# A two-block transformer kernel on one core: where the AdaLN weights are summed, and the order of small work around the norms

## The chip, the cores and the metric

One core of one Trainium2 chip runs the whole program; seven cores stand idle. The metric is device time in microseconds (us) of one execution, median of the runs shown. All times in this text are us, unless ns is written.

## The reference, cut to what matters

The input x has 256 tokens (S) of 1024 features (D). The first block is a hybrid layer: an RMS norm, three branches (A: a gated linear recurrence; B: a sparse attention with a compressed key branch and a relative position bias; C: a gated linear attention), each merged through its own weights and a sigmoid gate, an output projection `w_out`, a norm with residual, and a SwiGLU feed-forward layer. The second block has two layers (an "even" and an "odd" mixer) with a feed-forward layer ahead of each mixer and behind it, now on x and on 256 context tokens (512 in all, TOK). Each of its norms is modulated (AdaLN):

```
sc = jax.nn.silu(c)
scc = jax.nn.silu(c_ctx)
for li in range(DEPTH_2):
    m = jnp.split((sc @ ada_w[li] + ada_b[li])[:, None, :], N_MOD, axis=-1)
    mc = jnp.split(scc @ ada_w[li] + ada_b[li], N_MOD, axis=-1)
    h = half_ffn(h, norm_g[li, 0], m[0], m[1], m[2], ffn_w_gu[li, 0], ffn_w_down[li, 0])
def norm_mod(h, g, shift, scale):
    return rms_norm_2(h, g) * (1.0 + scale) + shift
```

So the vectors m and mc (shift, scale and gate of nine places, 9216 numbers a layer) are needed from the first feed-forward layer of the second block on.

## The kernel before, in words

**Products.** All large products are split in two: `hi` is a value rounded to fp32r, `lo` is the rest, and a product is three matmuls (hi x hi, hi x lo, lo x hi; lines 825 to 827, `split_part`; lines 874 to 876 where tokens stand on the partitions). Weights come in chunks of 2 MB (128 x 4096 fp32) through a ring of three slots (`NSLOT`). A chunk is two *halves* of 128 x 2048. For each half ScalarE makes the high part (`w_hi`, line 1336) and VectorE the rest (`w_lo`, line 1744); then TensorE computes two tiles of 128 features x 256 tokens from it, 48 matmuls of 256 columns. There are three buffers for high parts (`NHI`), so `w_hi(h)` waits until TensorE is done with half h-3, and the engines run two halves ahead of TensorE.

**Queues.** `make_plan` writes down stages, tiles and chunks in the order of the program; every engine walks the same order. SyncE (SP) issues the chunk loads (line 629): chunk i waits until what stood in its slot, chunk i-3, has been used. Tiles go through four banks of psum, so a tile waits until the tile four before it has been emptied, by ScalarE or VectorE as the plan says.

**AdaLN sums.** The 75 MB of `ada_w` are read in 72 halves of 1 MB. For a half VectorE makes four (later two) multiply-and-sum instructions of 128 x 1024 (`ada_dots`, line 1894) against `cb`, the silu of c and c_ctx on all partitions; the product goes to psum and the sum to `mod`. The first six halves are three chunks in the weight ring itself, one behind the first weight chunk of each merge A, C, B (`ADA_IN_MERGES`, `ada_in_merge`). The others have two buffers of their own (`ADA_BUF`), are loaded by SP between the chunks of the feed-forward layers (line 618) and are summed beside them (`ADA_BESIDE`: layer, step i, half). `mods` adds the bias and makes the scales and gates.

**Norms.** ScalarE squares (line 1343), TensorE sums over the partitions with a matrix of ones (line 789: eight matmuls, where q is in `PE_SUM`; else VectorE adds the squares in `rr`, line 1754, and one matmul sums, lines 793 and 804), ScalarE takes the root (1351, 1372), VectorE the reciprocal (1761), then eight pairs of `z` (1773 or 1814) and its rest (1782 or 1784), between which ScalarE makes the high part (1361).

**Tail and head.** At the end of feed-forward layers 1, 2, 3 and of the even mixer, `tail` computes the last two weight halves first for x and then for the context, `norm_total` sums the x squares, and `head` starts the next product with the x tokens. The weight rests of the second halves of those heads (`LO_BY_POOL`) are made by GpSimd (POOL, line 700), the others by VectorE.

**Start.** The compressed branch's bias (`cbias`, line 924: 15 small matmuls each) is made around the first norm. `cb` is loaded at the start by POOL. POOL also makes the parts of y and a (lines 660, 663, 715, 717) and, behind merge C's begin, loads `B_stage` (2 MB out of a DRAM scratch, line 683). VectorE makes the compressed blocks (line 2305) behind merge C; TensorE's `cmp_hid` (line 1171) waits for them.

## Time and profile before

| | |
|---|---|
| runs | 2574.13, 2575.12, 2575.86; median 2575.12 |
| profiled execution, its own time | 2577.12 |
| its span | 2575.3 |
| granted TensorE clock, mean | 0.956 |
| busy: PE, PEld, DVE, ACT, POOL | 2384.5, 2060.8, 1566.9, 873.3, 390.3 |
| HBM read | 351.15 MB |

PE is TensorE's matmuls, PEld its weight loads beside them, DVE VectorE, ACT ScalarE, POOL GpSimd, SP SyncE, whose DMA queue is SPq. Busy times are of the span. The granted clock is 1.0 at 2.4 GHz and 0.5 at 1.2 GHz. Idle time in brackets stands ahead of the instruction behind which it is written, with what ended it.

### The profile page before, as it was taken

To read this page: it belongs to the slowest core of one execution; us is meant where nothing else is said; L and a number is where in the kernel's file an instruction comes from. 1 tells how busy PE (TensorE), PEld (TensorE's weight loads), DVE (VectorE), ACT (ScalarE), POOL (GpSimd) and SP (SyncE) were. 2 spreads that over 40 slices of the span, in tenths; PEclk is the share of its full clock that TensorE was granted. 3 is DMA by queue.
4 is the path that set the end of the run, shared out by engine and by line. 5 is a ranking of instruction groups with operands and counts; after the bars stand their busy time and mean duration, and the time that the engine had idled before them with its cause. 6 is when DMAs were issued, how large, how long until landed. Compare 5 with 4: busy or idle time off the path is not lost.

```text
span 2575.3 us, 33604 instructions
## 1 busy us (share of the span) xinstructions
PE 2384.5 (93%) x14398; PEld 2060.8 (80%) x14398; DVE 1566.9 (61%) x1942; ACT 873.3 (34%) x1241; POOL 390.3 (15%) x349
## 2 busy tenths in 40 slices
PE   8898986777999999999989999999999999898999
PEld 7797873567989888888866888888888887777999
DVE  5585444655676887854774687733865533584554
ACT  5643322533434312222434421212422212344432
POOL 0020000102221121200011131301131201201111
PEclk9999997788999999999989999999999999899999
DMA  5443352023554455532320344422454322421453
GB/s 212 180 164 140 130 213 98 1 111 136 211 215 153 162 193 196 196 123 74 115 70 1 113 185 193 164 98 82 149 196 179 147 85 98 129 98 66 164 178 117
DMA packets 34257, 356.29 MB, mean 138 GB/s; under 512 B 3917, under 2 KB 6124, under 8 KB 8380
## 3 DMA queue, kind: packets, MB, share of 16 engines
q1 hardware_dynamic: 31212, 343.67, 35.9%
q0 software_dynamic: 2896, 10.46, 1.5%
q8 instruction: 114, 1.87, 0.3%
q14 instruction: 35, 0.29, 0.0%
HBM read 351.15 MB, written 1.13 MB: 137 GB/s over the span
## 4 chain that ended last, share of the span: by engine, by line
PE 78%; DVE 12%; DMA 4%; ACT 3%; issue 2%; POOL 1%; SPq 0%; DVEq 0%; ACTq 0%; POOLq 0%
PE psum L825 23%; PE psum L826 23%; PE psum L827 23%; DMA ring<-in_w 2%; PE psum L1120 2%; DVE ring_r L1744 1%; DVE arena L2335 1%; DVE zT L1773 1%; DMA arena<-in_w 1%; DVE psum L1894 1%; ACT arena_r L1336 1%; PE psum L1145 1%; PE psum L1115 1%; DVE rr L1761 1%; PE psum L789 1%
## 5 line engine op out<-in xcount | busy, mean ns | idle before, releaser
L825 PE MATMUL psum<-arena_r 128*128 128x256 f32 (+1 forms) x3368 | 1135.7, 337 | 54.3 <-DVE zT_r L1784 25.8
L827 PE MATMUL psum<-arena_r,ring_r 128*128 128x256 f32 (+1 forms) x3368 | 1125.0, 334 | 0.0
L826 PE MATMUL psum<-zT_r,arena_r 128*128 128x256 f32 (+1 forms) x2640 | 869.3, 329 | 0.0
L1336 ACT ACTIVATE arena_r<-ring 128x2048 fp32r<-128x2048 f32 (+1 forms) x252 | 473.9, 1881 | 912.2 <-PE psum L827 776.3
L825 PEld LDWEIGHTS psum<-arena_r 128*128 128x128 f32 x3368 | 642.0, 191 | 133.3 <-issue 33.7
L1744 DVE TENSOR_TENSOR ring_r<-ring,arena_r 128x2048 fp32r<-128x2048 f32 (+1 forms) x248 | 588.7, 2376 | 259.8 <-ACT arena_r L1336 258.6
L827 PEld LDWEIGHTS psum<-arena_r,ring_r 128*128 128x128 f32 x3368 | 643.6, 191 | 69.3
L826 PEld LDWEIGHTS psum<-zT_r,arena_r 128*128 128x128 f32 x2640 | 511.0, 194 | 46.1
L826 PE MATMUL psum<-arena_r 128*128 128x256 f32 (+1 forms) x1304 | 424.2, 325 | 0.0
L1894 DVE CUSTOM_DVE_ANT_0 psum<-arena,cb 128x1024 f32<-128x1024 f32 x232 | 328.0, 1470 | 14.3 <-DMA arena<-in_w 14.3
L826 PEld LDWEIGHTS psum<-arena_r 128*128 128x128 f32 x1304 | 246.7, 189 | 20.1
L825 PE MATMUL psum<-xT_r,arena_r 128*128 128x256 f32 x512 | 149.7, 292 | 39.8 <-DVE ring_r L1744 39.8
L715 POOL CAST arena_r<-rt 128x512 fp32r<-128x512 f32 (+1 forms) x55 | 53.5, 973 | 849.3 <-DVE rt L1956 849.3
L1829 DVE SCALAR_TENSOR_TENSOR xT<-psum,gates_h,xT 128x256 f32<-128x256 f32 x168 | 74.9, 478 | 140.8 <-PE psum L827 140.5
L827 PE MATMUL psum<-xT_r,ring_r 128*128 128x256 f32 x512 | 147.0, 287 | 0.0
L825 PEld LDWEIGHTS psum<-xT_r,arena_r 128*128 128x128 f32 x512 | 100.6, 196 | 44.6 <-issue 41.9
L1956 DVE TENSOR_TENSOR rr<-psum,rr 128x512 f32<-128x512 f32 (+1 forms) x55 | 32.1, 583 | 147.0 <-PE psum L827 147.0
L1956 DVE TENSOR_TENSOR rt<-psum,rt 128x512 f32<-128x512 f32 (+1 forms) x55 | 32.1, 583 | 134.7 <-PE psum L827 132.8
L1319 ACT ACTIVATE arena<-psum 128x256 f32<-128x256 f32 (+3 forms) x98 | 39.3, 409 | 200.5 <-PE psum L827 138.2
L715 POOL CAST arena_r<-rr 128x512 fp32r<-128x512 f32 (+1 forms) x55 | 53.7, 977 | 344.0 <-DVE rr L1956 344.0
L827 PEld LDWEIGHTS psum<-xT_r,ring_r 128*128 128x128 f32 x512 | 100.5, 196 | 0.0
L717 POOL TENSOR_TENSOR arena_r<-rr,arena_r 128x512 fp32r<-128x512 f32 (+1 forms) x55 | 85.5, 1554 | 4.4
(288 smaller groups left out, 2230.0 us busy)
## 6 DMA issues: line engine op xcount, KB each, us to landing
ring<-in_wf SPq DMA_DIRECT2D x75, 2048.0 KB, 7.8
ring<-in_w SPq DMA_DIRECT2D x45, 2048.0 KB, 8.0
arena<-in_w SPq DMA_DIRECT2D x66, 1024.0 KB, 9.8
ring<-in_wf SPq DMA_DIRECT2D x10, 1536.0 KB, 6.6
ring<-in_w SPq DMA_DIRECT2D x3, 1024.0 KB, 4.9
arena<-strip_scratch POOLq DMA_DIRECT2D x1, 2048.0 KB, 16.9
arena<-rpb_scratch POOLq DMA_DIRECT2D x16, 128.0 KB, 8.3
xT<-in_x SPq DMA_DIRECT2D x1, 1024.0 KB, 6.1
```

The costliest lines, as they stand in the source:

```text
L715: pool.tensor_copy(hi[:, i, :], a).then_inc(sig("a_hi"), 1)
L717: pool.tensor_tensor(out=lo[:, i, :], in0=a, in1=hi[:, i, :].bitcast(f32), op=ALU.subtract)\
L825: mm(b[c][:, at], whc, xh[:, k, at], start=(k == ks[0]), stop=False)
L826: mm(b[c][:, at], whc, xl[:, k, at], start=False, stop=False)
L827: last = mm(b[c][:, at], wlc, xh[:, k, at], start=False, stop=(k == ks[-1]))
L1120: last = mm(pt[:, r * P:(r + 1) * P], Pb[:, at:at + P], diag, start=True, stop=True)
L1319: A(dst(j), b[0:rows, 0:nt], func, scale=scale).then_inc(evac["A"], 1)
L1336: A(W_hi[h % NHI][:, 0:n], ring[:, half_slot(h)], ACT.Identity).then_inc(sig("w_hi"), 1)
L1744: v.tensor_tensor(out=ring_r[:, at], in0=ring[:, at], in1=W_hi[h % NHI][:, 0:HALVES[h][2]].bitcast(f32), op=ALU.subtract)\
L1829: return v.scalar_tensor_tensor(out=xT[:, k, at], in0=b[:, at], scalar=gate(k, s), in1=xT[:, k, at], op0=ALU.mult, op1=ALU.add)
L1894: v.tensor_tensor_reduce(out=psum[:, at:at + D], in0=src[:, b * D:(b + 1) * D], in1=cb[:, s * D:(s + 1) * D], scale=1.0, scalar=0.0, op0=A ...
L1956: v.tensor_tensor(out=a, in0=b[:, 0:nt], in1=a, op=ALU.mult).then_inc(evac["V"], 1)
```

## The change

- **AdaLN halves.** None goes through the ring any more. Halves 0 and 1 are loaded behind the last chunk of merge B and summed while `w_out` is computed. Halves 2 to 7 are summed beside feed-forward layer 0 at the same steps as six halves were before, but are loaded earlier (`ADA_LOADS`: up to two chunks ahead). Layer 1 takes 28 halves in place of 24, at steps 0 to 27. `mods` for the first norm makes shift and scale first, the gates at step 4 of layer 1.
- **cb.** Its load goes behind POOL's parts of branch A, its silu behind `nsa_q1`.
- **Start.** Both `cbias` go behind `small`, ahead of the LRU gates. `w_hi(0)` and `w_hi(1)` stand ahead of the high parts of z, and `w_lo(0)` stands between the reciprocal and the first z.
- **Gates.** ScalarE empties the tiles of `lru_g3` and `small` before `w_hi` of `gla_q0` and `gla_q1`.
- **Compressed blocks** are made inside merge C, behind its second chunk; POOL's load of `B_stage` waits until the first half of merge C's last chunk is done.
- **norm1** is summed by VectorE and one matmul, its squares made during `w_out`.
- **Tails.** `norm_total(q, 0)` goes between the two tiles of the context's first half; the reciprocal goes ahead of `c_part(5)`; VectorE makes all rests, that of the head's second half behind the eight z of x; ScalarE makes its high part behind the first four high parts of z.
- M_hi moves in the arena, so that `ADA_BUF` is free at `w_out`.

```diff
-ADA_BESIDE = {0: {2 + 3 * i: 6 + i for i in range(6)}, 1: {i: 12 + i for i in range(24)},
+ADA_BESIDE = {0: {2 + 3 * i: 2 + i for i in range(6)}, 1: {i: 8 + i for i in range(28)},
               2: {i: 36 + i for i in range(18)}, 3: {i: 54 + i for i in range(18)}}
+ADA_LOADS = {1: (2,), 2: (3,), 4: (4,), 6: (5,), 7: (6,), 9: (7,), 10: (8,), 12: (9,)}
...
             split(f"merge{br}{c}_0", f"merge{br}{c}_1", w8(at + c), "AA", who2="VV")
-            if c == 0:
-                add(f"ada{ada}", w8(W8_ADA + ada), "", "ada")
...
     merge("B", W8_MERGE_B)
+    ada_half(0)
+    ada_half(1)
     split_pairs("w_out", 2, W8_OUT, "AA")
...
-                    if halves_sent >= 2 * ADA_IN_MERGES + 2:
+                    if halves_sent >= 2:
                         sp.wait_ge(sig("ada_dots"), dots_before(halves_sent - 1))
...
+            pool.wait_ge(filled, TILE["mergeC3_0"] + 2)
             src = bass.AP(tensor=strip_dram.tensor, offset=0, ap=[[1, P], [384, 16], [1, S]])
             pool.dma_start(B_stage, src).then_inc(sig("stage_in"), 16)
...
-                b0, b1 = half_banks(h), half_banks(h + 1)
-                split_part(h, b0, x_, xh, xl, sig("tail_x"), ks=ks)
-                split_part(h + 1, b1, x_, xh, xl, sig("tail_x"), ks=ks)
-                split_part(h, [high_bank(n), high_bank(n + 1)], c_, xh, xl, filled, ks=ks)
-                norm_total(q, 0)
+                split_part(h, half_banks(h), x_, xh, xl, sig("tail_x"), ks=ks)
+                split_part(h + 1, half_banks(h + 1), x_, xh, xl, sig("tail_x"), ks=ks)
+                split_part(h, [high_bank(n), high_bank(n + 1)], c_, xh, xl, filled, ks=ks,
+                           between=lambda: norm_total(q, 0))
...
-            norm(0, xT, lambda k: act.wait_ge(sig("x_in"), 16), middle=lambda: w_hi(0))
-            w_hi(1)
+            norm(0, xT, lambda k: act.wait_ge(sig("x_in"), 16), middle=lambda: (w_hi(0), w_hi(1)))
...
                 c_part(4)
+                recip_part(q, 0)
                 c_part(5)
-                w_lo(h + 3)
-                recip_part(q, 0)
...
                 z_parts(q, 0, between)
+                w_lo(h + 3)
                 recip_part(q, 1)
...
-            evac_pairs("lru_g", 4, lambda c: copy_tiles(f"lru_g{c}", 2, lambda j: A_g[:, 2 * c + j, :],
-                                                        func=ACT.Gelu_apprx_tanh))
-            w_hi(HALF_AT["small"] + 2)
+            evac_pairs("lru_g", 3, lru_g)
+            lru_g(3)
             b = empty(TILE["small"])
             A(C_lr, b[64:80, 0:S], ACT.Identity)
             A(C_gate, b[0:48, 0:S], ACT.Sigmoid).then_inc(evac["A"], 1)
+            w_hi(HALF_AT["gla_q0"])
+            w_hi(HALF_AT["gla_q1"])
...
             for c in range(4):
                 lo(f"w_out{c}")
+                if c in (1, 2):
+                    ada_half(c - 1)
+            for k in range(1, 6):
+                add_square(1, k, HALF_TOK[0])
```

How the order of the instructions moves is shown at three places. Line numbers are those of each kernel: 1744 before is 1740 now (weight rest), 1761 is 1757 (reciprocal), 1773, 1784 are 1769, 1780 (z and its rest), 1754 is 1750 (adding squares), 629 is 633 (ring load), 618 is 622 (AdaLN load).

SP's loads from the fourth chunk to feed-forward layer 0, before:

```order
L629 DMA ring<-in_w 128x4096 x30
L629 DMA ring<-in_wf 128x4096 x4
L618 DMA arena<-in_w 128x2048
L629 DMA ring<-in_wf 128x4096
L618 DMA arena<-in_w 128x2048
L629 DMA ring<-in_wf 128x4096 x2
L618 DMA arena<-in_w 128x2048
```

and of the change:

```order
L633 DMA ring<-in_w 128x4096 x25
L622 DMA arena<-in_w 128x2048 x2
L633 DMA ring<-in_w 128x4096 x2
L633 DMA ring<-in_wf 128x4096 x2
L622 DMA arena<-in_w 128x2048
L633 DMA ring<-in_wf 128x4096
L622 DMA arena<-in_w 128x2048
L633 DMA ring<-in_wf 128x4096 x2
```

The ring has three loads of 2 MB less before the feed-forward layer; two small loads stand behind merge B, and the next ones after its second and third chunk in place of its fourth and fifth.

VectorE between the last z of x and the first z of the context in the first tail and head, before:

```order
L1784 SCALAR_TENSOR_TENSOR zT_r<-zT,mod,arena_r 128x256
L1754 TENSOR_TENSOR rr<-rr,zT 128x256 x4
L1773 SCALAR_TENSOR_TENSOR zT<-xT,modA,rr 128x256
L1784 SCALAR_TENSOR_TENSOR zT_r<-zT,mod,arena_r 128x256 x3
L1761 RECIPROCAL rr<-rt 128x256
L1773 SCALAR_TENSOR_TENSOR zT<-xT,modA,rr 128x256 x3
```

and of the change:

```order
L1750 TENSOR_TENSOR rr<-rr,zT 128x256 x4
L1769 SCALAR_TENSOR_TENSOR zT<-xT,modA,rr 128x256
L1780 SCALAR_TENSOR_TENSOR zT_r<-zT,mod,arena_r 128x256 x3
L1740 TENSOR_TENSOR ring_r<-ring,arena_r 128x2048
L1757 RECIPROCAL rr<-rt 128x256
L1769 SCALAR_TENSOR_TENSOR zT<-xT,modA,rr 128x256 x3
```

The rest of the head's second half, on POOL before (line 700), stands ahead of the context's reciprocal.

VectorE at the start, before:

```order
L2004 COPY cmp_bias<-psum 128x15x16
L2010 MEMSET arena 128x8x3
L2011 MEMSET mod 128x288
L1761 RECIPROCAL rr<-rt 128x256
L1814 SCALAR_TENSOR_TENSOR zT<-xT,vec,rr 128x256 x3
```

and of the change:

```order
L2008 MEMSET arena 128x8x3
L2009 MEMSET mod 128x288
L1757 RECIPROCAL rr<-rt 128x256
L1740 TENSOR_TENSOR ring_r<-ring,arena_r 128x2048
L1812 SCALAR_TENSOR_TENSOR zT<-xT,vec,rr 128x256 x3
```

The first weight rest goes ahead of the z, which it followed, and the bias copy has left the start.

## Rows read from the trace of the kernel before

**Rows 1.** The waits of PE in the whole run: total, times, longest.

```profile
PE psum L825 <- DVE ring_r L1744: 45.5, 10, 9.2
PE psum L825 <- DVE zT_r L1784: 25.8, 10, 4.2
```

**Rows 2.** Windows: merges A, C, B; C's first chunk. Length, busy, PEclk, DMA share, GB/s.

```profile
174.10:232.30 58.20, 48.55 (x388) 48.03 (x388) 38.06 (x39) 23.40 (x22) 0.00 (x0) 0.91 0.47 181
324.90:386.90 62.00, 49.21 (x387) 48.48 (x385) 29.08 (x36) 15.13 (x15) 5.85 (x9) 0.92 0.60 221
533.80:591.50 57.70, 47.62 (x388) 47.26 (x387) 34.38 (x39) 18.03 (x17) 9.50 (x10) 0.91 0.43 165
324.90:336.50 11.60, 11.57 (x99) 11.36 (x97) 2.82 (x3) 4.42 (x5) 5.85 (x9) 1.00 0.97 300
```

**Rows 3.** Timeline, merge A's last chunk: its load issued, its high part.

```profile
206.26 4.30 SPq L629 DMA_DIRECT2D ring<-in_w  x3
...
214.11 1.91 ACT L1336 ACTIVATE arena_r<-ring 128x2048 fp32r<-128x2048 f32 x1 [15.61 <-DMA ring<-in_w]
```

**Rows 4.** Timeline, merge C's third chunk, and the way to the compressed hidden layer.

```profile
336.50 0.33 SPq L629 DMA_DIRECT2D ring<-in_w  x1
...
348.81 1.91 ACT L1336 ACTIVATE arena_r<-ring 128x2048 fp32r<-128x2048 f32 x1 [10.11 <-DMA ring<-in_w]
...
402.75 4.28 DVE L2305 TENSOR_TENSOR arena<-arena,vec 128x120 f32<-128x120 f32 x16
...
405.03 15.35 PE L1171 MATMUL psum<-ring,arena 128*60 128x256 f32 x64 [18.17 <-DVE arena L2305]
```

**Rows 5.** Timeline, the start up to the first weight product.

```profile
7.77 2.56 ACT L1343 ACTIVATE zT<-xT 128x256 f32<-128x256 f32 x8 [4.29 <-DMA xT<-in_x]
...
11.62 5.50 PE L789 MATMUL psum<-zT,cst 128*128 128x256 f32 x16
...
19.52 1.28 DVE L1814 SCALAR_TENSOR_TENSOR zT<-xT,vec,rr 128x256 f32<-128x256 f32 x3
...
25.38 4.48 DVE L1744 TENSOR_TENSOR ring_r<-ring,arena_r 128x2048 fp32r<-128x2048 f32 x2
...
27.92 0.55 PE L825 MATMUL psum<-xT_r,arena_r 128*128 128x256 f32 x1 [7.36 <-DVE ring_r L1744]
```

**Rows 6.** Timeline, the LRU gates: ScalarE's wait, TensorE's, and VectorE behind the last gate.

```profile
83.04 1.91 ACT L1336 ACTIVATE arena_r<-ring 128x2048 fp32r<-128x2048 f32 x1 [12.91 <-DMA ring<-in_w]
...
85.28 2.07 PE L953 MATMUL psum<-arena,ring 128*128 128x256 f32 x4 [6.66 <-ACT arena L1319]
...
97.97 2.29 DVE L2056 TENSOR_TENSOR arena<-arena 128x2048 f32<-128x2048 f32 x1 [8.35 <-ACT arena L1497]
```

**Rows 7.** Timeline, norm1's sum on TensorE.

```profile
621.93 5.38 PE L789 MATMUL psum<-zT,cst 128*128 128x256 f32 x16 [2.38 <-ACT zT L1343]
```

**Rows 8.** Timeline, feed-forward layer 0: an AdaLN sum's wait, two idles of TensorE.

```profile
701.64 1.23 DVE L1894 CUSTOM_DVE_ANT_0 psum<-arena,cb 128x1024 f32<-128x1024 f32 x1 [5.10 <-DMA arena<-in_w]
...
709.39 0.36 PE L825 MATMUL psum<-arena_r 128*128 128x256 f32 x1 [1.96 <-DVE arena L1963]
...
745.44 0.35 PE L825 MATMUL psum<-arena_r 128*128 128x256 f32 x1 [2.40 <-DVE rr L1956]
```

**Rows 9.** Timeline, the tail of layer 1 and the head behind it.

```profile
1217.84 0.43 DVE L1754 TENSOR_TENSOR rr<-rr,zT 128x256 f32<-128x256 f32 x1 [0.22 <-ACT zT L1343]
...
1220.80 0.60 PE L804 MATMUL psum<-rr,cst 128*128 128x256 f32 x2
...
1223.73 5.56 DVE L1773 SCALAR_TENSOR_TENSOR zT<-xT,modA,rr 128x256 f32<-128x256 f32 x3
...
1223.79 4.82 POOL L700 TENSOR_TENSOR ring_r<-ring,arena_r 128x2048 fp32r<-128x2048 f32 x1 [31.10 <-ACT arena_r L1336]
...
1229.83 0.35 PE L825 MATMUL psum<-arena_r 128*128 128x256 f32 x1 [4.18 <-DVE zT_r L1784]
...
1238.39 0.59 PE L804 MATMUL psum<-rr,cst 128*128 128x256 f32 x2
```

More of the change, by code:

```diff
@@ L224, in make_plan @@
     split_pairs("gla_og", 2, W8_OG, "AA")
-    merge("A", W8_MERGE_A, 0)
+    merge("A", W8_MERGE_A)
     add("gla_t", None, "AA")
@@ L233, in make_plan @@
     add("gla_y1", None, "VV")
-    merge("C", W8_MERGE_C, 1)
+    merge("C", W8_MERGE_C)
     for i in range(2):
@@ L239, in make_plan @@
     add("cmp_kv", None, "VV")
-    merge("B", W8_MERGE_B, 2)
+    merge("B", W8_MERGE_B)
+    ada_half(0)
+    ada_half(1)
     split_pairs("w_out", 2, W8_OUT, "AA")
@@ L483, in build @@
         B_T = area(B_T_at, 16, S)
-        M_hi = part(6144, KT, S)
+        M_hi = part(11264, KT, S)
         K_tbl = rt[:, S:S + 16]
@@ L945, in _ @@
             last.then_inc(filled, 1)
+            cbias(0)
+            cbias(1)
             w = get("lru_gates").rearrange("p (g n e) -> p g n e", g=2, n=8)
@@ L1636, in _, with w_out @@
             merge("B")
-            evac_pairs("w_out", 4, lambda c: copy_tiles(f"w_out{c}", 2, lambda j: Y_y[:, 2 * c + j, :]))
-            norm(1, Y_y, lambda k: wait_evac(act, TILE["w_out0"] + k))
+            def w_out(c):
+                copy_tiles(f"w_out{c}", 2, lambda j: Y_y[:, 2 * c + j, :])
+                for k in range(max(0, 2 * c - 2), 2 * c):
+                    wait_evac(act, TILE["w_out0"] + k)
+                    square(1, k, HALF_TOK[0], Y_y, "norm_sq")
+            evac_pairs("w_out", 4, w_out)
+            norm(1, Y_y, lambda k: wait_evac(act, TILE["w_out0"] + k), squared=6)
             norm(2, xT, lambda k: act.wait_ge(sig("norm_x"), k + 1))
@@ L1806, in norm @@
                 recip(HALF_TOK[0])
+                if middle is not None:
+                    middle()
                 if q == 9:
@@ L1975, in ffn, with merge @@
                         if i == 18:
-                            mods(0, 0)
+                            mods(0, 0, 0, 16, with_gate=False)
                         ctx_norm(i)
-            def merge(br, ada):
+                    if f == 1 and i == 4:
+                        mods(0, 0, 16, 24, with_scale=False)
+            def merge(br, after=None):
                 for c in range(4):
@@ L1994, in merge @@
                             v.tensor_tensor(out=m, in0=m, in1=mg_t[:, j, :], op=ALU.add).then_inc(evac["V"], 1)
-                    if c < 2:
-                        ada_in_merge(2 * ada + c)
+                    if c == 1 and after is not None:
+                        after()
             b = empty(TILE["strip"])
@@ L2049, in _ @@
             dve.wait_ge(sig("cst_rest_in"), 16)
-            for c in range(1, 4):
-                lo(f"lru_g{c}")
+            lo("lru_g1")
+            lo("lru_g2")
+            cbias(0)
+            cbias(1)
+            lo("lru_g3")
             lo("small")
@@ L2136, in _ @@
             v.tensor_copy(C_e, C_b).then_inc(sig("gla_kend"), 1)
[L2137 to L2138 removed]
+            merge("A")
             link(v.memset(C_at, 0.0))
@@ L2197, in _, with blocks @@
             gla_low(1)
-            merge("C", 1)
+            def blocks():
+                for i in range(2):
+                    pos = V("pos_k" if i == 0 else "pos_v")
+                    dve.wait_ge(sig("stack_in"), 8 * 16)
+                    for g in range(4):
+                        st = B_st_at + (4 * i + g) * S
+                        for half in range(2):
+                            at = st + 16 * half
+                            src = arena[:, at:at + 240].rearrange("p (c m two) -> p m c two", m=8, two=2)[:, :, :, 0]
+                            last = v.tensor_tensor(out=B_bl[:, i, 8 * half:8 * half + 8, g * CMP_N:(g + 1) * CMP_N],
+                                                   in0=src, in1=rep(pos[:, 8 * half:8 * half + 8], CMP_N), op=ALU.add)
+                        last.then_inc(sig("cmp_blocks"), 1)
+            merge("C", blocks)
             def att_max(u):
@@ L2293, in attention @@
                     att_done(u, y)
-            for i in range(2):
-                pos = V("pos_k" if i == 0 else "pos_v")
-                dve.wait_ge(sig("stack_in"), 8 * 16)
-                for g in range(4):
-                    st = B_st_at + (4 * i + g) * S
-                    for half in range(2):
-                        at = st + 16 * half
-                        src = arena[:, at:at + 240].rearrange("p (c m two) -> p m c two", m=8, two=2)[:, :, :, 0]
-                        last = v.tensor_tensor(out=B_bl[:, i, 8 * half:8 * half + 8, g * CMP_N:(g + 1) * CMP_N],
-                                               in0=src, in1=rep(pos[:, 8 * half:8 * half + 8], CMP_N), op=ALU.add)
-                    last.then_inc(sig("cmp_blocks"), 1)
             for i in range(8):
```

116 lines of the change are left out of this document (48 added, 68 removed).

## The prediction

> **What bounds the kernel now.** I began with the page: TensorE is busy for 2384.5 of 2575.3 (the table), so the kernel is a chain of matmuls with some 190 of idle time, and a change that leaves the matmuls as they are can only take idle time and time at the low clock. The waits say what ends TensorE's idle time [rows 1]: weight rests (line 1744) for 45.5 in ten waits, the longest 9.2, and the rests of z for 25.8 in ten. Both are places that the change touches. The windows [rows 2] price the first: a merge is four chunks, one clean chunk takes 11.6 at a granted clock of 1.00, so a merge should take 46.4; they take 58.2, 62.0 and 57.7, at 0.91 to 0.92.
>
> The cause is in the timeline. The last chunk of merge A was issued at 206.26, right when VectorE was done with the AdaLN sums of the ring's extra chunk; its high part could begin only at 214.11 [rows 3], when TensorE was idle already. The slot was held by AdaLN weights, not by merge weights. The other big idle times are read from rows 4 to 9, in the order of the steps.
>
> **Step 1, no AdaLN chunk in the ring.** Each merge chunk then waits for merge weights alone, is issued a chunk of TensorE's work (11.6) earlier than now, and needs some 8 to land (206.26 to 214.11, rows 3) plus the high part (1.91) and the rest (half of 4.48, rows 5): 12 of the two chunks, 23, that lie between issue and use. So the idle goes, and with it the stretch at 1.2 GHz that follows each one. Merge A gains 58.2 - 46.4 less 0.8 for a wait at its second chunk on the gate chain, which is not about loads: 11.0. Merge C gains 62.0 - 46.4 = 15.6, merge B 57.7 - 46.4 = 11.3. Sum 37.9. Below 0 I see nothing; the upper end is 38.7.
>
> The dots themselves (24 instructions) move to `w_out` and to steps 24 to 27 of layer 1, where a half has 512 tokens and lasts TensorE as long as a clean chunk here, 11.6, and VectorE has a rest, a product and four sums of 1.23 [rows 8]: hidden. At `w_out` they are counted in step 5. The move of `cb` costs nothing: the load is needed some 80 later, and ScalarE has half of each weight half free at `nsa_q1`.
>
> **Step 2, compressed blocks inside merge C.** TensorE waited 18.17 for them [rows 4]. They took 2.3 of that to their fourth row; ahead of them VectorE and ScalarE both stood at the weight half of merge B, whose load is issued only when merge C ends. That stays: ScalarE makes this high part ahead of the sigmoid that empties the bank `cmp_hid` needs. So the new wait is a load, 1.91 and 0.4. The load takes 8 alone (rows 3), but 12.3 beside POOL's `B_stage` (336.50 to 348.81, rows 4), and the change puts `B_stage` at half a chunk ahead of this very load. I take 12.3, the row of the same collision: wait 14.7, gain 3.5. Ends: 0 (more than sharing) and 8.
>
> **Step 3, the start.** The sum of norm0 now begins at 11.62, behind `cbias`; the squares begin at 7.77 [rows 5]. It could begin 3.5 sooner, but earlier in the time at the low clock that every start shows, so I take 2.2. The first product waits for its weight rest, which stands behind all z, 8.4 from the first z (19.52) to 27.92. Now the rest (2.24) goes first, and the product starts with the first z rest, 1.7 behind the first z: 3.9 and 0.3 of waits. Gain 4.2. VectorE's z and rests (about 0.4 each) then keep ahead of matmuls at the low clock. Sum 6.4; ends 2 (the clock comes later for want of early work) and 8.
>
> **Step 4, the gates.** TensorE waited 6.66 there, then again for the sigmoid's table, because ScalarE held two ready tiles behind a high part whose weights landed at 83.04 [rows 6]. Now the tiles go first, and the two `cbias` (3.5 each) stand in this time; the gates' own emptying starts when both high parts are done (about 8.8 after `small`) and takes 16 by 0.45. Together 16.0. Now VectorE sees the last gate at 97.97 [rows 6], 19.4 to 19.9 after the 78.1 at which `small` ends (85.28 less 6.66 and the 0.6 of two gate rows ahead of it): 3.4. Ends 0 and 5.
>
> **Step 5, norm1.** Sixteen rows take 5.38 [rows 7]; one product like that of line 804 takes 0.60 [rows 9]. The upper end is 4.8. VectorE comes late, though: behind the last high part of `w_out` it has a weight rest, the sums of half 1 and another rest, then five adds and two. I find it about 2.7 behind the last square, so 2.1. Lower end -2.
>
> **Step 6, layer 0.** A sum waits 5.10 for its load, and VectorE being in order the weight rest behind it is late: idle of 1.96 at 709.39, later 2.40 at 745.44 [rows 8], and a stretch at 1.2 GHz behind the second that costs 1.7. The loads now go up to two chunks sooner, so 6.1. Ends 0 and 6.1.
>
> **Step 7, the four tails.** At layer 1's end the sum of squares is ready at 1218.27 but TensorE takes it at 1220.80 [rows 9], behind both context tiles. Between the tiles it goes at 1218.8: the reciprocal 2.0 sooner. Then the striking row: three z take 5.56, where three took 1.28 at the start [rows 5, 9]. In just that time POOL makes the weight rest (4.82). So VectorE stands still for 4.3, and a rest of 2.29 on VectorE is the cheaper one. The Trainium skill ("Perfetto Trace Analysis", section "Optimizing Scalar/DVE Operations") says that where DVE is saturated it may make sense to offload work, even to GpSimd; by that rule taking it back would cost a rest at each of four places, though the same section warns that the two share a port and it might not help. The trace bears out the warning, not the offload.
>
> Both together would give 6.4, but the x chain then meets TensorE: `c_part(7)` stands in VectorE's queue behind the fourth z and waits for the tail's last tile, 1225.65 (1229.83 less 4.18). From there 0.5, then four z and six rests of 0.4 and four adds of 0.43 with their waits bring the last rest at about 1232.1, and TensorE ends the first half at 1233.4, against 1238.39: 5.0 gained. The moved rest (2.29) begins at 1232.1 and ends at 1234.4, so TensorE idles about 0.9 where it did not: 4.1. Layers 2 and 3 read the same; behind layer 3 the next weights stand behind VectorE's context z anyway, so the 0.9 is not paid twice: 5.0. The mixer's tail has longer context tiles that hide more of the stall already; I take 2.8. Sum 4.1 + 2.8 + 4.1 + 5.0 = 16.0. Ends 8 and 20.
>
> **Sum.** 37.9 + 3.5 + 6.4 + 3.4 + 2.1 + 6.1 + 16.0 = 75.4 off the profiled execution's 2577.1 gives 2501.7. That execution was 2.0 above the median, so in terms of the median 2499.7; I say 2500.
>
> **The rivals.**
> (a) The merges gain little, because another wait takes over (ScalarE's gate tiles, POOL's shares, or `B_stage` and `cb` in the way of the loads). For it: the DMA share in merge C's first chunk is already 0.97 at 300 GB/s [rows 2]. Against: that chunk held the stage load, and the others did not. With half of step 1 gone and step 2 at 0: 2500 + 19 + 3.5 = 2522; with all of step 1 gone 2541.
> (b) VectorE is the full engine in the heads and POOL the free one: the slow z come from something else, as from the context squares beside them, and VectorE pays a rest of 2.3 in each head for nothing. Then step 7 gives -9 in place of 16: 2525. (That is what the page's offload rule would make of it.) Against it: POOL's row and the long z coincide to 0.1.
> (c) Slower than before. SP has one queue. An AdaLN load that waits for sums holds every ring load behind it, which is what cost merge A its 8 of idle and some 3 of low clock. In layer 0 each load from half 4 on waits for the half two before it, and halves 6 and 8 have about half a weight half (6) of margin. If VectorE's sums run later than that, each blocked load costs about 11; from seven such loads on, of some 30, the gain of 75 is gone, and with ten the time is 2612. Against: the same rule of two buffers runs in layers 1 to 3 now, with no idle to show for it.
> (d) The change doesn't do what it says: merge chunks still come late, since ScalarE and VectorE in order make the parts only two halves ahead. Then the loads land early and nothing follows; the price is that of (a) in full, 2541. The row at 214.11, which was waiting for DMA and not for TensorE, speaks against it.
>
> **How the numbers follow.** The forecast has 0.70, its own range 2488 to 2512 from the ends of steps 2 to 7. (a) with half 0.12, (b) 0.06, (a) or (d) in full 0.05, (c) 0.03, and 0.04 for more than I count (2480). The range 2485 to 2530 leaves out the full (a), (c) and the lowest. A measurement here tells about 0.2% (5) from no change. Faster by over 0.2%: 0.95; within: 0.02; slower: 0.03.
>
> **What would show it.** Right: merges of 46 to 47 at a clock near 1.00; the wait ahead of line 1171 near 15; the first product near 21.5; three z in each head in 1.3; no AdaLN sum waiting for DMA in layer 0. Wrong: ring loads that follow AdaLN sums in SP's row, z rows that are still long, idle ahead of the second half of each head of over 2, or a `cmp_hid` that waits for 18 or more. If the total falls by under 45, step 1 failed.

## The result, and the profile after

| | before | after |
|---|---|---|
| runs | 2569.6, 2574.13, 2575.12, 2575.86 | 2482.93, 2483.65, 2485.07, 2487.62 |
| median | 2574.62 | 2484.36 |
| profiled execution, span | 2575.3 | 2481.0 |
| granted TensorE clock, mean | 0.956 | 0.969 |
| time at half clock | 231 | 158 |

The kernel before has one run more here (2569.6). The ratio, of the means, is 0.9655 (95% interval 0.9643 to 0.9668); the medians differ by 90: faster. The forecast said 2500 with a range of 2485 to 2530, so the median lies 0.6 outside the range's lower end, and that end lies well within the interval (some 2482 to 2489). The span shrank by 94.3, where the sum of the steps said 75.4. The page of the changed kernel, its line 1 and two groups of its part 5 (the busy engines; then busy time, mean ns | idle before, releaser):

```profile
PE 2354.6 (95%) x14384; PEld 2034.6 (82%) x14384; DVE 1565.3 (63%) x1954; ACT 873.7 (35%) x1241; POOL 378.1 (15%) x345
...
L1740 DVE TENSOR_TENSOR ring_r<-ring,arena_r 128x2048 fp32r<-128x2048 f32 (+1 forms) x252 | 595.2, 2363 | 214.3 <-ACT arena_r L1325 213.1
L1892 DVE CUSTOM_DVE_ANT_0 psum<-arena,cb 128x1024 f32<-128x1024 f32 x256 | 363.7, 1479 | 0.0
```

VectorE now makes all 252 rests, and no AdaLN sum waits for anything (the 0.0). PE's busy time fell by 30. Of this 4.2 is the sum of norm1 (sixteen matmuls in 5.38 before, two in 1.19 now); the products are the same, and fewer of them ran at the low clock. The waits of PE:

```profile
PE psum L817 <- DVE zT_r L1780: 14.4, 6, 4.2
...
PE psum L1161 <- ACT rt L1446: 11.6, 1, 11.6
...
PE psum L817 <- DVE ring_r L1740: 6.9, 6, 5.1
```

Waits for weight rests fell from 45.5 to 6.9 (against [rows 1]), 5.1 of it in one place that comes up below. The merges A, C, B, in the columns of [rows 2]:

```profile
165.38:211.90 46.52, 45.82 (x388) 45.64 (x387) 28.68 (x23) 23.67 (x22) 0.00 (x0) 1.00 0.50 181
304.53:350.04 45.51, 45.51 (x387) 45.31 (x385) 24.14 (x36) 15.58 (x15) 5.87 (x9) 1.00 0.69 231
489.25:535.00 45.75, 45.75 (x389) 45.75 (x388) 25.34 (x23) 18.60 (x18) 9.67 (x10) 1.00 0.57 207
```

All three run at a granted clock of 1.00, two without any idle time. SP's waits of the kernel before (in total, times, longest) say what had held the ring loads:

```profile
SPq L629 <- DVE mod L1894: 65.5, 3, 24.9
```

Three ring loads, one a merge, waited for AdaLN sums (`mod`). In the changed kernel no ring load waits for a sum. Next the way to the compressed hidden layer (SP, ScalarE, TensorE), to be held against [rows 4]:

```profile
338.73 11.68 SPq L633 DMA_DIRECT2D ring<-in_w  x2
...
359.35 1.91 ACT L1325 ACTIVATE arena_r<-ring 128x2048 fp32r<-128x2048 f32 x1 [24.09 <-DMA ring<-in_w]
...
361.68 16.33 PE L1161 MATMUL psum<-ring,arena 128*60 128x256 f32 x64 [11.64 <-ACT rt L1446]
```

The wait is 11.64 and no longer for VectorE's blocks but for a sigmoid (L1446) behind the high part of merge B's first chunk. That load was issued at 350.07 (the second of the two) and had landed by 359.35. The start, to be held against [rows 5]:

```profile
8.23 5.27 PE L781 MATMUL psum<-zT,cst 128*128 128x256 f32 x16 [2.00 <-ACT zT L1332]
...
15.77 3.71 ACT L1325 ACTIVATE arena_r<-ring 128x2048 fp32r<-128x2048 f32 x2 [1.76 <-DMA ring<-in_w]
...
17.79 2.29 DVE L1740 TENSOR_TENSOR ring_r<-ring,arena_r 128x2048 fp32r<-128x2048 f32 x1 [1.92 <-ACT arena_r L1325]
...
21.75 0.55 PE L817 MATMUL psum<-xT_r,arena_r 128*128 128x256 f32 x1 [8.25 <-DVE zT_r L1778]
```

And the tail of layer 1 with its head, VectorE and TensorE, to be held against [rows 9]:

```profile
1153.34 1.75 DVE L1757 RECIPROCAL rr<-rt 128x256 f32<-128x256 f32 x1 [0.85 <-ACT rt L1340]
...
1155.53 1.26 DVE L1769 SCALAR_TENSOR_TENSOR zT<-xT,modA,rr 128x256 f32<-128x256 f32 x3
...
1164.57 0.39 PE L817 MATMUL psum<-arena_r 128*128 128x256 f32 x1 [1.55 <-DVE zT_r L1780]
...
1166.79 0.59 PE L796 MATMUL psum<-rr,cst 128*128 128x256 f32 x2
...
1167.66 0.36 PE L817 MATMUL psum<-arena_r 128*128 128x256 f32 x1 [0.27 <-DVE ring_r L1740]
```

Three z take 1.26 where they took 5.56, and the idle of 4.18 at the head's start is gone; a new one of 1.55 stands ahead of the last matmuls of its first half.

**Where the time came from.** I counted the matmuls of the split products (3944 of line 825, now line 817) and took for the same one its time before less its time after, at the borders of the steps:

| part | forecast | measured |
|---|---|---|
| 3 start | 6.4 | 6.6 |
| 4 gates | 3.4 | 2.1 |
| 1 merges A, C, B | 11.0, 15.6, 11.3 | 11.6, 16.4, 12.1 |
| 2 from merge C to merge B | 3.5 | 7.7 |
| 5 w_out, norm1, norm2 | 2.1 | 2.5 |
| 6 layer 0 | 6.1 | 6.4 |
| 7 tails of layer 1, even mixer, layers 2, 3 | 4.1, 2.8, 4.1, 5.0 | 5.9, 4.6, 5.9, 6.2 |
| even and odd mixer, last layer | 0 | 2.7, 4.2, -1.1 |

### The profile page after: what moved, and what is told of

It is laid out like the page before. It is cut to its first block, busy times and chain, and to the rows that moved or that the text cites. A ratio compares the mean times of both kernels' runs of the same rounds, so it can differ in the third digit from the quotient of the medians.

```text
span 2481.0 us, 33593 instructions
## 1 busy us (share of the span) xinstructions
PE 2354.6 (95%) x14384; PEld 2034.6 (82%) x14384; DVE 1565.3 (63%) x1954; ACT 873.7 (35%) x1241; POOL 378.1 (15%) x345
## 2 busy tenths in 40 slices
DMA packets 34689, 356.29 MB, mean 144 GB/s; under 512 B 3965, under 2 KB 6172, under 8 KB 8428
## 4 chain that ended last, share of the span: by engine, by line
PE 83%; DVE 10%; ACT 3%; issue 2%; DMA 1%; POOL 1%; SPq 0%; DVEq 0%; ACTq 0%
PE psum L817 25%; PE psum L818 24%; PE psum L819 24%; PE psum L1110 2%; DVE ring_r L1740 2%; DVE arena L2340 1%; DMA ring<-in_w 1%; DVE rr L1750 1%; PE psum L1161 1%; ACT arena L1588 1%; PE psum L1105 1%; PE psum L1079 1%; PE psum L1135 1%; PE psum L1015 1%; ACT arena_r L1325 1%
## 5 line engine op out<-in xcount | busy, mean ns | idle before, releaser
L1740 DVE TENSOR_TENSOR ring_r<-ring,arena_r 128x2048 fp32r<-128x2048 f32 (+1 forms) x252 | 595.2, 2363 | 214.3 <-ACT arena_r L1325 213.1
L818 PEld LDWEIGHTS psum<-zT_r,arena_r 128*128 128x128 f32 x2640 | 503.5, 191 | 46.0
L1892 DVE CUSTOM_DVE_ANT_0 psum<-arena,cb 128x1024 f32<-128x1024 f32 x256 | 363.7, 1479 | 0.0
L817 PEld LDWEIGHTS psum<-xT_r,arena_r 128*128 128x128 f32 x512 | 97.0, 189 | 12.7 <-issue 12.6
## 6 DMA issues: line engine op xcount, KB each, us to landing
arena<-strip_scratch POOLq DMA_DIRECT2D x1, 2048.0 KB, 11.6
arena<-rpb_scratch POOLq DMA_DIRECT2D x16, 128.0 KB, 11.3
```

What stands on the lines that cost most here:

```text
L817: mm(b[c][:, at], whc, xh[:, k, at], start=(k == ks[0]), stop=False)
L818: mm(b[c][:, at], whc, xl[:, k, at], start=False, stop=False)
L1740: v.tensor_tensor(out=ring_r[:, at], in0=ring[:, at], in1=W_hi[h % NHI][:, 0:HALVES[h][2]].bitcast(f32), op=ALU.subtract)\
L1892: v.tensor_tensor_reduce(out=psum[:, at:at + D], in0=src[:, b * D:(b + 1) * D], in1=cb[:, s * D:(s + 1) * D], scale=1.0, scalar=0.0, op0=A ...
```

## The experiments

Names that begin with b_ are edits of the kernel before, a_ undo one part of the changed kernel, x_ go on from it. "Later" and "sooner" are against the changed kernel's trace at the same matmul.

**b_ring_out: steps 1 and 6 alone.**

```diff
-            if c == 0:
-                add(f"ada{ada}", w8(W8_ADA + ada), "", "ada")
...
     merge("B", W8_MERGE_B)
+    ada_half(0)
+    ada_half(1)
...
+ADA_LOADS = {1: (2,), 2: (3,), 4: (4,), 6: (5,), 7: (6,), 9: (7,), 10: (8,), 12: (9,)}
```

> The kernel before with steps 1 and 6 of the prediction alone: no AdaLN chunk in the ring, the earlier AdaLN loads of layer 0; start, gates, blocks, norm1, tails and the weight rests on POOL as before. Theory (ring slots held by AdaLN weights make the late loads): merges A, C, B fall to about 46.5 each, 40 less in all, layer 0 gains 6, sum 46: 2529, and the wait ahead of the compressed hidden layer stays near 18. Rival (a) or (d) (parts come late anyway, the gain came from elsewhere): merges near 52 to 58, 2550 or more.

Measured 2524.19, ratio 0.9806 (0.9791 to 0.9820). Its merges, in the columns of [rows 2]:

```profile
174.04:220.50 46.46, 45.76 (x389) 45.59 (x388) 28.74 (x24) 23.65 (x22) 0.00 (x0) 1.00 0.51 182
313.02:358.50 45.48, 45.48 (x387) 45.30 (x385) 19.88 (x20) 15.56 (x15) 5.85 (x9) 1.00 0.73 255
506.36:552.10 45.74, 45.74 (x389) 45.74 (x388) 25.33 (x23) 18.59 (x18) 9.65 (x10) 1.00 0.57 208
```

The two steps give 50, more than half of the whole, without the help of any other. Rivals (a) and (d) fall. The edit takes the AdaLN weights out of the slots and their eight sums a merge off VectorE at once. That it is the slot and not VectorE's time is read from the trace: the high part of [rows 3] waited for DMA, and SP for the sums. Layer 0 is 11.1 shorter here, where I had expected 6: 5.2 of it is idle time, most of the rest clock (13.6 at half clock before, 5.4 here). In merge C the stage load still stood where it had been (the DMA share is 0.73), and the merge is as short all the same.

**b_dve_rest: only the rests taken from POOL.**

```diff
-        LO_BY_POOL = tuple(HEADS[q] + 1 for q in (5, 6, 7, 8))
...
-            w_lo(LO_BY_POOL[0])
```

> The kernel before with one edit: the rests of the heads' second halves are made by VectorE at their old place, ahead of the reciprocal, and not by POOL. Theory (POOL's 4.8 operation stops VectorE): the three z ahead of the fourth take 1.3 in place of 5.6, the idle of 4.18 at the end of the tails goes; the rest of 2.3 lies mostly in the wait for the root. 3 to 4 a head, 12 to 16 in all: 2559 to 2563. Rival (b) (something else slows z): z rows stay near 5.6 and VectorE has 2.3 more a head, 0 to 9 slower: 2575 to 2584.

Measured 2572.23, ratio 0.9996 (0.9987 to 1.0006): nothing. VectorE in the same tail:

```profile
1225.78 2.29 DVE L1725 TENSOR_TENSOR ring_r<-ring,arena_r 128x2048 fp32r<-128x2048 f32 x1 [2.26 <-ACT arena_r L1322]
1227.99 1.74 DVE L1742 RECIPROCAL rr<-rt 128x256 f32<-128x256 f32 x1
1229.77 1.28 DVE L1754 SCALAR_TENSOR_TENSOR zT<-xT,modA,rr 128x256 f32<-128x256 f32 x3
```

```profile
1231.59 0.36 PE L811 MATMUL psum<-arena_r 128*128 128x256 f32 x1 [3.90 <-DVE zT_r L1765]
```

The three z take 1.28, so POOL was what made them long. But the idle at the head's start is 3.90 where it was 4.18. A new wait took the old one's place: the rest stands ahead of the reciprocal and waits for its high part, which ScalarE makes only behind the root, ready at 1225.75. My expectation had put the rest into the wait for the root. The high part stands behind the root in ScalarE's queue, so the rest can't. Taking the rest back pays only together with the new places: the high part behind four z, the rest behind eight.

**a_pool_rest: the rests back on POOL, all else as changed.**

```diff
+            w_lo(LO_BY_POOL[0])
...
                 root(q, 0)
+                w_hi(h + 3)
...
                 z_high(q, 0, 0, 4)
-                w_hi(h + 3)
```

> The changed kernel with the rests of the four heads' second halves back on POOL, and ScalarE's high part of them back ahead of the z high parts; all else as changed. Theory: POOL's row is 4.8 again and stands beside VectorE's z, which take 5.6 for three again; the idle at the end of the tails is back, less the 1.5 that the rest on VectorE costs now: 3 a head, 10 to 14 in all, 2494 to 2498. Rival (b): z rows stay at 1.3 for three and the idle of 1.53 ahead of each second half goes: 2478 or less.

Measured 2498.07, ratio 0.9705 (0.9689 to 0.9721), as the theory said. POOL and VectorE in the first tail:

```profile
1157.10 4.56 POOL L706 TENSOR_TENSOR ring_r<-ring,arena_r 128x2048 fp32r<-128x2048 f32 x1 [29.57 <-ACT arena_r L1339]
```

```profile
1155.74 1.27 DVE L1788 SCALAR_TENSOR_TENSOR zT<-xT,modA,rr 128x256 f32<-128x256 f32 x3
1158.06 3.87 DVE L1799 SCALAR_TENSOR_TENSOR zT_r<-zT,mod,arena_r 128x256 fp32r<-128x256 f32 x1 [1.05 <-ACT arena_r L1364]
```

Three z that came before POOL's operation are short. The next instruction, of 0.48 elsewhere, takes 3.87 and ends 0.3 behind POOL's. So it isn't a z that is slow, but what VectorE begins while POOL runs. Not everything, though. In the changed kernel POOL still makes small parts, and at the end of merge B two products of VectorE begin beside them:

```profile
535.01 0.41 DVE L1992 TENSOR_TENSOR rt<-psum,rt 128x256 f32<-128x256 f32 x1
535.45 0.99 DVE L1993 TENSOR_TENSOR zT<-zT,rt 128x256 f32<-128x256 f32 x1
```

```profile
534.75 0.59 POOL L662 CAST arena_r<-zT 128x256 fp32r<-128x256 f32 x1
535.42 0.74 POOL L665 TENSOR_TENSOR zT_r<-zT,arena_r 128x256 fp32r<-128x256 f32 x1
```

The one that reads psum and one SBUF tensor keeps its 0.41; the one with two SBUF inputs, 0.42 elsewhere, takes 0.99 and ends 0.3 behind POOL's. The Trainium skill ("SBUF — State Buffer", section "Who interferes with whom") says that a VectorE instruction with two SBUF inputs contends with a GpSimd one that reads SBUF, and that the port pair which the two share is an exclusive lock; by that rule the trace agrees, in both kernels. The four tails are 3.4, 1.5, 3.3 and 3.6 longer, 11.8 together.

**a_total_late: the x sum back behind both context tiles.**

```diff
-                split_part(h, half_banks(h), x_, xh, xl, sig("tail_x"), ks=ks)
-                split_part(h + 1, half_banks(h + 1), x_, xh, xl, sig("tail_x"), ks=ks)
-                split_part(h, [high_bank(n), high_bank(n + 1)], c_, xh, xl, filled, ks=ks,
-                           between=lambda: norm_total(q, 0))
+                b0, b1 = half_banks(h), half_banks(h + 1)
+                split_part(h, b0, x_, xh, xl, sig("tail_x"), ks=ks)
+                split_part(h + 1, b1, x_, xh, xl, sig("tail_x"), ks=ks)
+                split_part(h, [high_bank(n), high_bank(n + 1)], c_, xh, xl, filled, ks=ks)
+                norm_total(q, 0)
```

> The changed kernel with the x sum of the tails back behind both context tiles. Theory (TensorE takes the sum 2.0 later, and all that follows in the x chain of VectorE moves with it): each tail and head 1.5 to 2 longer, 6 to 8 in all, 2491. Rival (the x chain then meets TensorE's last tile anyway, as c_part(7) stands in it, so the sooner sum is worth nothing): 2485.

Measured 2493.64 (profiled) and 2505.34, ratio 0.9713 (0.9659 to 0.9768), both above the 2491 that I expected; the profiled one is 10.8 longer in span. The tails are 2.7, 1.5, 3.8 and 2.7 longer, 10.7 in all, where I had said 6 to 8. The trace shows why; TensorE at the first tail's beginning:

```profile
1138.19 0.36 PE L817 MATMUL psum<-arena_r 128*128 128x256 f32 x1 [1.24 <-DVE xT L1828]
```

The same idle of 1.24 stands ahead of all four tails here, as in the kernel before (there 1206.7 to 1207.9), and ahead of none in the changed kernel. It comes from the line with `b0, b1`: `half_banks(h + 1)` waits until the second half's banks are empty, and it was called ahead of the first half's matmuls. The changed lines call it behind them. This is worth 1.4 a tail, 5.6 in all; the sum's place itself is worth 5.1. With the 11.8 of the rest these add up to 22.5, and the tails gained 22.6. Each part was undone alone, though, and b_dve_rest shows that the parts depend on each other, so the sum is a good sign rather than a proof of the shares.

**a_stage_early: no wait ahead of the stage load.**

```diff
-            pool.wait_ge(filled, TILE["mergeC3_0"] + 2)
             src = bass.AP(tensor=strip_dram.tensor, offset=0, ap=[[1, P], [384, 16], [1, S]])
```

> The changed kernel without POOL's wait for merge C's last chunk ahead of the stage load, which then stands behind the stack loads as before. Theory (ring loads that share the DMA engines with it take 12 in place of 8): a load inside merge C is late by 4 and TensorE idles 0 to 4 there, while the load behind merge C lands 1 sooner and the wait ahead of the compressed hidden layer falls from 11.6 to 10.5: 2483 to 2487. Rival (with a free ring the loads have over a chunk of margin): merge C stays at 45.5 and only the wait falls, 2482 to 2484.

Measured 2479.45 and 2484.81, ratio 0.9646 (0.9618 to 0.9674): the same as the changed kernel.

```profile
357.73 1.91 ACT L1324 ACTIVATE arena_r<-ring 128x2048 fp32r<-128x2048 f32 x1 [22.60 <-DMA ring<-in_w]
...
360.06 2.36 PE L1160 MATMUL psum<-ring,arena 128*60 128x256 f32 x5 [10.14 <-ACT rt L1445]
```

The load issued at 349.94 was used at 357.73, 7.8 later, where beside the stage load it was 9.3. So sharing costs this load 1.5, not the 4.3 of [rows 4]. There the stage load, held up by the stack loads ahead of it, was under way from 331.71 to 348.63, all through the ring load's 12.3; in the changed kernel it is issued at 344.69 and has landed at 356.29, beside two thirds of the 9.3. Merge C stays as short. The new wait is worth nothing.

**a_blocks_late: the compressed blocks behind merge C.**

```diff
-            merge("C", blocks)
+            merge("C")
...
```

The loop that makes the blocks stands ahead of the emptying of `flip` again, as in the kernel before.

> The changed kernel with the compressed blocks back behind merge C. Theory (step 2): VectorE makes them behind the rests of merge B's first half and the last products, so the wait ahead of the compressed hidden layer is 11.6 plus the rest of 2.3 and the blocks up to their fourth row, some 5 to 7 longer: 2489 to 2491. Rival (the blocks were never what ended that wait): 2484 to 2485.

Measured 2489.88 and 2496.68, ratio 0.9690 (0.9672 to 0.9707).

```profile
373.44 16.55 PE L1161 MATMUL psum<-ring,arena 128*60 128x256 f32 x64 [19.55 <-DVE arena L2303]
```

The wait is 7.9 longer (5 to 7 expected), so the blocks' place is what counts, and the span from merge C's begin to merge B's 8.4 longer. 4.0 of this run's time was lost earlier, at the gates, where the two kernels are the same (see below).

**a_late_loads: the AdaLN loads of layer 0 at their old chunks.**

```diff
-ADA_LOADS = {1: (2,), 2: (3,), 4: (4,), 6: (5,), 7: (6,), 9: (7,), 10: (8,), 12: (9,)}
+ADA_LOADS = {3: (2,), 4: (3,), 6: (4,), 7: (5,), 9: (6,), 10: (7,), 11: (8,), 12: (9,)}
```

> The changed kernel with the AdaLN loads of feed-forward layer 0 back at the chunks where they stood before (the third, fourth, sixth and so on, in place of the first, second, fourth). Theory (a sum of VectorE that waits for its load delays the weight rest behind it): a sum waits 5 for DMA again, idle of 2.0 and 2.4 is back in layer 0, 4 to 6 longer: 2489 to 2491. Rival (c) in small (the early loads hold ring loads behind sums that run late): 2480 or less.

Measured 2489.07 and 2496.05, ratio 0.9686 (0.9653 to 0.9720).

```profile
683.79 1.23 DVE L1892 CUSTOM_DVE_ANT_0 psum<-arena,cb 128x1024 f32<-128x1024 f32 x1 [5.03 <-DMA arena<-in_w]
...
691.67 0.36 PE L817 MATMUL psum<-arena_r 128*128 128x256 f32 x1 [2.27 <-DVE rr L1953]
```

The wait of 5 is back, and with it the idle behind it; layer 0 is 219.5 long, 4.1 longer than in the changed kernel, and its idles over 0.3 add up to 11.7 where they were 7.8. (Layer 0 takes from 211.7 to 215.4 over the kernels that share its code, so the 4.1 is rough and could be up to 7.8; the idle time is the firmer number.) The early loads hold nothing up. (5.1 more were lost at the gates in the profiled run, again where the kernels are the same.)

**a_start_back and a_gates_back: steps 3 and 4 undone, one at a time.**

```diff
-            norm(0, xT, lambda k: V("norm_g", k, 1), middle=lambda: w_lo(0))
+            cbias(0)
+            norm(0, xT, lambda k: V("norm_g", k, 1))
+            w_lo(0)
...
-            cbias(0)
-            cbias(1)
```

The second `cbias(1)` goes behind `w_lo(1)`, and the plan, TensorE and ScalarE get their old order of the start back.

> The changed kernel with step 3 undone: both bias stages around the first norm again, the first weight rest behind all z; the order at the gates as changed. Theory (steps 3 and 4 add up): the first product 6.2 later at 27.9; at the gates TensorE now idles where the two bias stages (3.5 each at the low clock, less at the high) filled the wait, but the gates end as ScalarE sets them, so the shift ahead of merge A stays 6 to 7: 2491. Rival (the start only moves the wait to the gates or the gate chain): shift ahead of merge A under 3, 2487 or less.

Measured 2488.60 and 2489.09, ratio 0.9672 (0.9644 to 0.9700): the first product is 7.3 later and merge A begins 7.4 later; in the end 6.1 are left. (The 3.5 of a bias stage, in the expectation and in steps 3 and 4, is at the full clock and not at the low one: the second of the kernel before took 3.52 from 17.05 on, where the granted clock is 1.00.)

```diff
-            evac_pairs("lru_g", 3, lru_g)
-            lru_g(3)
+            evac_pairs("lru_g", 4, lru_g)
+            w_hi(HALF_AT["small"] + 2)
...
-            w_hi(HALF_AT["gla_q0"])
-            w_hi(HALF_AT["gla_q1"])
```

> The changed kernel with step 4's order on ScalarE undone: the high parts of the next two halves ahead of the tiles of the last gate product and of the small one; the bias stages stay ahead of the gates. Theory (the two tiles wait behind a high part whose weights land late): TensorE idles 3 to 6 at the gates, but as ScalarE's emptying of the gates ends only 2 sooner by the change, 2 to 3 longer in all: 2486 to 2487. Rival (the bias stages' place alone gave the gain): 2484.

Measured 2489.55 and 2490.88, ratio 0.9678 (0.9660 to 0.9695). TensorE idles 3.65 among the bias stages, and merge A begins 7.0 later, more than either theory said. But merge A also began 3.0, 5.1 and 4.0 later in the profiled runs of x_evac_od, a_late_loads and a_blocks_late, whose edits all lie behind merge A. The same window of the changed kernel and of two of these, in the columns of [rows 2]:

```profile
60.00:165.00 105.00, 100.41 (x773) 97.86 (x773) 74.30 (x59) 60.27 (x81) 18.33 (x17) 0.95 0.48 177
```

```profile
60.00:165.00 105.00, 100.64 (x747) 97.55 (x746) 71.86 (x58) 59.84 (x80) 18.34 (x17) 0.92 0.46 174
```

```profile
60.00:165.00 105.00, 100.65 (x745) 97.56 (x744) 71.85 (x58) 59.17 (x79) 18.32 (x17) 0.92 0.46 170
```

One code, two granted clocks: the stretch at half clock behind `small` is 6.8 in some runs and 13.7 in others. a_gates_back had the long one, so 2 to 4 of its 7.0 are the edit's; whether the edit also makes the long one likelier stays open.

**a_norm1_pe: step 5 undone.**

```diff
-        PE_SUM = (0, 2, 4)
-        SUMS = (1, 3, 5, 6, 7, 8, 9), (4, 5, 6, 7, 8)
+        PE_SUM = (0, 1, 2, 4)
+        SUMS = (3, 5, 6, 7, 8, 9), (4, 5, 6, 7, 8)
...
```

The squares go behind `w_out` on ScalarE, and VectorE's adds go.

> The changed kernel with step 5 undone: the squares of norm1 behind w_out and summed by sixteen matmuls of TensorE. Theory (VectorE's seven adds behind two AdaLN halves come 4.6 late, sixteen rows take 5.4 and start 2.4 late): 2 longer, 2486. Rival (the time of the adds is the time of the matmuls): 2484.

Measured 2482.25 and 2482.73, ratio 0.9648 (0.9630 to 0.9665), no difference from the changed kernel. At its place the step is worth 1.5 (layer 0 begins 1.5 later), but it is gone again by the second layer's end, 0.7 and 1.0 of it where stretches at half clock fell shorter. As a total it can't be told from nothing.

**x_evac_first: the last tiles of merge C emptied first.** The profile after left one long wait, 11.64 for a sigmoid whose two tiles had been ready since 344, and which stood in ScalarE's queue behind a high part whose load could only be issued when merge C ended.

```diff
                     h, n = HALF_AT[f"merge{br}{c}_0"], TILE[f"merge{br}{c}_0"]
-                    w_hi(h + 2)
+                    late = br == "C" and c == 3
+                    if not late:
+                        w_hi(h + 2)
...
+                    if late:
+                        w_hi(h + 2)
                     w_hi(h + 3)
```

with the same for VectorE's two rests and its products.

> The changed kernel with one order turned at merge C's last chunk: ScalarE's two sigmoids and VectorE's products of that chunk go ahead of the high parts and rests of merge B's first chunk. Theory (the wait of 11.64 ahead of the compressed hidden layer is for a bank that ScalarE empties only behind the high part of a chunk whose load is issued when merge C ends): the wait falls to about 1, 10 less, 2474. Rival (the weights of the hidden layer, loaded beside the stage load, land late, or the wait comes back ahead of merge B or cmp_turn): a gain under 4, 2480 or more.

Measured 2469.40, ratio 0.9590 (0.9575 to 0.9604): faster than the changed kernel by 15.

```profile
344.30 0.39 ACT L1448 ACTIVATE rt<-psum 128x256 f32<-128x256 f32 x1 [2.47 <-PE psum L819]
358.93 3.71 ACT L1325 ACTIVATE arena_r<-ring 128x2048 fp32r<-128x2048 f32 x2 [14.24 <-DMA ring<-in_w]
```

```profile
349.84 14.02 PE L1161 MATMUL psum<-ring,arena 128*60 128x256 f32 x64
```

The wait is gone entirely, and the 64 matmuls behind it take 14.02 where they took 16.33, since TensorE comes to them without a pause and at the high clock. The 3.71 of high parts now lie under the hidden layer.

**x_evac_od: the same, and one rest sooner behind layer 3.** The other long wait for a rest, the 5.1 of the wait list:

```profile
2137.05 0.77 PE L817 MATMUL psum<-arena_r 128*128 128x512 f32 x1 [5.08 <-DVE ring_r L1740]
```

```diff
                 recip_part(q, 1)
+                if q == 8:
+                    w_lo(h + 4)
                 z_parts(q, 1)
```

> The changed kernel with merge C's last tiles emptied first, as in the run before of that edit, and one more order turned: behind layer 3 the rest of the next half (the odd mixer's second) goes ahead of VectorE's z of the context, which need 6.4. Theory (TensorE's idle of 5.08 behind the odd head's first half is for that rest, whose high part is ready 6 sooner): the idle goes, 5 less than with the first edit alone, 2464. Rival (the context's z come 2.3 later and TensorE then waits for them): 0 to 2 less, 2468.

Measured 2465.25, ratio 0.9583 (0.9570 to 0.9596), the fastest of all.

```profile
2119.27 2.29 DVE L1744 TENSOR_TENSOR ring_r<-ring,arena_r 128x2048 fp32r<-128x2048 f32 x1 [0.67 <-ACT arena_r L1325]
```

```profile
2123.29 0.47 PE L817 MATMUL psum<-arena_r 128*128 128x512 f32 x1 [0.82 <-DVE zT_r L1784]
```

0.82 of the idle is left, now for a z rest. The matmul behind it comes 4.3 sooner, and at the odd mixer's end 4.9 are left. The medians differ by 4 (the intervals overlap); that this edit helps rests on this place of the trace more than on the times.

## Why the prediction was right, and where it fell short

The parts of the table above add up to 93.8, 18.4 more than the 75.4 of the forecast. Step 7 has 6.6 of this, the mixers and the last layer 5.8, step 2 4.2 and step 1 2.2; the others have -0.4 together.

- **Step 1 (37.9, measured 40.1)** held in mechanism and size, and b_ring_out shows it alone. The clean chunk is 11.4, not the 11.6 that I read off merge C's first chunk, which gives the 2.2.
- **Step 2 (3.5, measured 7.7)** had the right wait: "a load, 1.91 and 0.4". Mis-sized was the load: I took the 12.3 of [rows 4], and it was 9.3; a_stage_early has 7.8 for the free one. The wait was 11.64 where I said 14.7. The other 1.2 I had no term for: the remaining idle times up to merge B are 2.4 shorter and the matmuls there 1.3 longer, 1.0 of it in the hidden layer (16.33 where it was 15.35).
- **Step 3 (6.4, measured 6.6).** The sum did start 3.4 sooner, and it took 5.27 where it had taken 5.50, so what I took off for the low clock wasn't lost. What I missed is that the high part then waited 1.76 for its weights, and VectorE 1.92 for the high part: of the sum's 3.6 only 1.7 was left, where I had 2.2. The order of the rest gave 4.4, where I had 4.2. That the total fits is in part luck, as one error hid the other. The first product is at 21.75, said 21.5.
- **Step 4 (3.4, measured 2.1).** The high parts were done at 80.3, as I said (8.8 after `small`), but the two bias stages took 8.6 and not 7: the first 3.5 at full clock, the second 5.1, 3.8 of it at half clock. ScalarE could begin with the first gate at 81.3.
- **Step 5 (2.1, measured 2.5 with both norms)** is 1.5 at its place by a_norm1_pe, and nothing in the total.
- **Step 6 (6.1, measured 6.4)** held in the sum; a_late_loads gives 4.1 for the loads. The idles of 1.96 and 2.40 are gone; a third, for POOL's share, is there before and after (2.81 and 2.50).
- **Step 7 (16.0, measured 22.6) is the step that failed.** "From there 0.5, then four z and six rests" was right: from the tail's last tile to the context's sum I said 5.0 less, and it is 4.9 (from 12.7, 1225.65 to 1238.39, to 7.8, 1159.0 to 1166.8). But I costed the moved sum and not the line that moved with it. `half_banks(h + 1)` had been called ahead of the first half, with an idle of 1.24 at each tail, and the diff shows the call move. The missing term is 1.4 four times, 5.6; 1.0 of the 6.6 stays without a cause. The new idle ahead of the second half was said as 0.9 and is 0.3; the 1.55 stands a little earlier, behind the four adds.
- **The mixers and the last layer (0, measured 5.8).** No edit touches them. In the even mixer 16 matmuls behind the same idle of 2.49, of the kernel before and of the changed one:

```profile
1395.16 3.78 PE L1120 MATMUL psum<-arena 128*128 128x128 f32 x16 [2.49 <-DVE arena L2273]
```

```profile
1323.46 2.05 PE L1110 MATMUL psum<-arena 128*128 128x128 f32 x16 [2.49 <-DVE arena L2285]
```

  The idle times are the same within 0.2 (13.4 and 13.2 in the even mixer's part, 15.1 and 15.0 in the odd one's), but the time at half clock fell from 20.5 to 10.2 and from 22.9 to 15.4. Over the kernels that share this code these parts vary by up to 4, so this is nothing that the change does by itself. It is luck, and without these 5.8 the time would lie inside the range.
- **The rivals.** (a) and (d) fell with b_ring_out, (b) with a_pool_rest, (c) with a_late_loads and the changed trace: in layer 0 each of SP's early loads is issued directly behind the ring load ahead of it (the first at 608.46, with that load's issue over at 608.41). The offload rule of the Trainium skill ("Perfetto Trace Analysis", section "Optimizing Scalar/DVE Operations") would have kept the rests on POOL; a_pool_rest measures that as 14 slower, so the section's warning holds and not its offer.

So steps 1, 2, 4 and 6 held in mechanism, step 3 missed a load, step 5 can't be told from nothing, and step 7 lacked a term. The direction stood, and the range was too narrow on its low side: it had room for errors of the terms I had, and little for a term that I hadn't seen.

## What to carry to other kernels

- A ring slot lent to side data delays a load three chunks later, not at its own place; look at what stood in the slot of the load that comes late. And a consumer in order holds all behind it: an emptying that is ready should not queue behind a part whose load is not even issued.
- An operation on POOL beside VectorE's chain isn't free: where VectorE's next instruction reads two SBUF inputs, count the whole length as a stop. But moving it back pays only where its input is ready and nothing urgent stands behind it.
- When lines are rewritten around a moved call, read what each expression waits for when it is evaluated. And between two profiled runs don't read differences of a few us in places that no edit touched: compare the same place over several kernels.
